# A fused encoder layer with 32 experts: down-projection chunks placed between gate/up chunks, and both gather halves through one pair of PSUM banks

## What is computed

```python
def moe(h, w_router, b_router, w_gu, b_gu, w_down, b_down):
    logits = (xt @ w_router + b_router).astype(jnp.float32)
    top_vals, top_idx = lax.top_k(logits, TOP_K)          # 4 of 32 experts
    gates = jax.nn.softmax(top_vals, axis=-1).astype(h.dtype)
    ...
    def expert_block(args):
        gu = xblk @ w_gu[e] + b_gu[e]                     # 1024 -> 2048
        x_glu = jnp.minimum(gu[:, :F], SWIGLU_LIMIT)
        x_lin = jnp.clip(gu[:, F:], -SWIGLU_LIMIT, SWIGLU_LIMIT)
        act = x_glu * jax.nn.sigmoid(SWIGLU_ALPHA * x_glu) * (x_lin + 1.0)
        return act @ w_down[e] + b_down[e]                # 1024 -> 1024
    ...
y = rms_norm(x + moe(rms_norm(x, norm_ffn_w), ...), norm_final_w)
```

## Time and profile before

| | us |
|---|---|
| median of 3 runs | 1229.29 (1227.29 to 1232.49) |
| the profiled execution | 1230.21 |
| its span, first to last instruction | 1228.4 |
| PE busy in the span | 1147.9 (93%) |
| DVE busy | 1102.8 (90%) |
| ACT busy | 923.5 (75%) |
| weights and other data moved | 457.80 MB, mean 373 GB/s |

### The profile page before, as it was taken

How to read it: one execution, slowest core, us unless ns; L and a number is a source line. 1 busy time by engine, 2 the same in 40 slices (tenths; PEclk the granted TensorE clock), 3 DMA queues, 4 the chain that set the end, 5 groups by cost and what they waited for, 6 DMA issues and landing times.

```text
span 1228.4 us, 40032 instructions
## 1 busy us (share of the span) xinstructions
PE 1147.9 (93%) x17576; PEld 888.3 (72%) x17577; DVE 1102.8 (90%) x804; ACT 923.5 (75%) x825; POOL 92.2 (8%) x69
## 2 busy tenths in 40 slices
PE   5999999899999999999999999999999999999995
PEld 3444655877878878887877777777777787887852
DVE  5855576989999999999999999999999999999987
ACT  4435345778888888888888888888888888888861
POOL 0110400000240000000000000000000000000320
PEclk9999999999999999999999999999999999999998
DMA  9504873999999999999999999999999999999983
GB/s 348 215 23 172 293 289 148 396 398 408 417 420 420 421 419 421 420 420 420 420 419 420 418 420 420 419 418 419 418 415 416 414 417 420 420 420 403 421 343 160
DMA packets 73143, 457.80 MB, mean 373 GB/s; under 512 B 10034, under 2 KB 10546, under 8 KB 23520
## 3 DMA queue, kind: packets, MB, share of 16 engines
q1 hardware_dynamic: 68480, 445.30, 88.7%
q0 software_dynamic: 3360, 7.93, 1.7%
q10 hardware_dynamic: 1152, 2.19, 0.5%
HBM read 443.26 MB, written 24.38 MB: 381 GB/s over the span
## 4 chain that ended last, share of the span: by engine, by line
PE 81%; DVE 9%; issue 6%; DMA 2%; ACT 2%; DVEq 0%; SPq 0%; ACTq 0%
PE ps L445 36%; PE ps L482 24%; PE ps L1155 8%; PE ps L438 6%; DVE ring L423 4%; PE ps L1258 2%; PE ps L467 1%; DMA arena<-planes 1%; DMA ring<-in_w_in_dram 1%; PE ps L1195 1%; PE ps L1183 1%; DVE arena L1895 0%; DVE ring L1516 0%; DVE arena L1901 0%; PE ps L452 0%
## 5 line engine op out<-in xcount | busy, mean ns | idle before, releaser
L445 PE MATMUL ps<-arena,ring 128*128 128x88 f16 x12288 | 500.5, 205 | 36.5 <-issue 35.2
L445 PEld LDWEIGHTS ps<-arena,ring 128*128 128x128 f16 x12288 | 487.6, 100 | 43.0 <-issue 40.0
L423 DVE SCALAR_TENSOR_TENSOR ring<-ring 128x2048 f16<-128x2048 f32 x196 | 439.6, 2283 | 3.5 <-ACT ring L420 2.9
L423 DVE SCALAR_TENSOR_TENSOR ring<-arena,ring 128x2048 f16<-128x2048 f32 x156 | 353.8, 2286 | 32.1 <-ACT ring L420 32.1
L420 ACT ACTIVATE ring<-ring 128x2048 f16<-128x2048 f32 x196 | 365.1, 1908 | 11.0 <-DMA ring<-in_w_gu_dram 5.0
L482 PE MATMUL ps<-ring,arena 128*88 128x512 f16 x1536 | 337.2, 379 | 0.8 <-issue 0.7
L420 ACT ACTIVATE ring<-arena 128x2048 f16<-128x2048 f32 x156 | 291.1, 1904 | 5.0 <-DMA arena<-in_w_down_dram 2.2
L482 PEld LDWEIGHTS ps<-ring,arena 128*88 128x88 f16 x1536 | 181.9, 120 | 142.3 <-issue 1.1
L504 POOL DMA_INDIRECT planes<-arena,slot_row x30 | 66.4, 2213 | 938.3 <-ACT arena L529 909.1
L529 ACT ACTIVATE arena<-ps,slot_gate 88x512 f32<-88x512 f32 x60 | 37.8, 680 | 94.3 <-PE ps L482 94.3
L438 PE MATMUL ps<-arena 128*128 128x88 f16 x2048 | 92.9, 205 | 10.8 <-issue 10.4
(11 more groups left out here) (171 smaller groups left out, 628.4 us busy)
## 6 DMA issues: line engine op xcount, KB each, us to landing
ring<-in_w_gu_dram SPq DMA_DIRECT2D x130, 1024.0 KB, 19.7
arena<-in_w_gu_dram SPq DMA_DIRECT2D x125, 1024.0 KB, 18.8
ring<-in_w_down_dram SPq DMA_DIRECT2D x66, 1024.0 KB, 19.3
extra<-in_w_down_dram SPq DMA_DIRECT2D x31, 1024.0 KB, 20.3
arena<-in_w_down_dram SPq DMA_DIRECT2D x31, 1024.0 KB, 19.7
ring<-in_w_in_dram SPq DMA_DIRECT2D x4, 2048.0 KB, 12.5
ring<-in_w_out_dram SPq DMA_DIRECT2D x2, 2048.0 KB, 8.5
arena<-planes SPq DMA_DIRECT2D x4, 1024.0 KB, 14.5
```

The costliest lines, as they stand in the source:

```text
L423: return dve.scalar_tensor_tensor(split_of(slot)[:, 1, :], raw(r), SCALE_W, split_of(slot)[:, 0, :], ALU.mult, ALU.subtract)
L445: mm = pe.matmul(o, w[:, i, cols], src[:, j, k, :], start=start and n == 0, stop=stop and n == 2, skip_group_check=True)
```

## The change

The 12 chunks of a stage get a new order, `ORDER`: g0, g1, g2, d0, g3, d1, g4, g5, d2, g6, g7, d3. Loads, `high`, `low` and PE's products all follow it. The silu and the clamp of an expert, which read the finished gate/up sums, now wait for the first 11 chunks of its stage (`GU_END`) and stand in the next stage: ACT's silu behind high 3, DVE's clamp behind low 3. The product follows low 4 and its low part follows low 5; on ACT the rows and the product's high part stand between high 4 and high 5. Both gather halves go through banks 6 and 7 (`MISC`); PE waits before the second until ACT has copied the first. The first two experts' first halves still go through banks 4 and 5 (`BOTH[1]`). Stage 1, written out by hand before, becomes an ordinary stage.

```diff
+    ORDER = ("g0", "g1", "g2", "d0", "g3", "d1", "g4", "g5", "d2", "g6", "g7", "d3")
+    GU_END = 11
...
             def place(h, q, c):
                 s = 2 * h + q
                 slot = raw_slot(h, q, c)
-                ins = load_gu(sp, c, s, slot) if c < GU_CH else load_dn(sp, c - GU_CH, s - 1, slot)
+                k = int(ORDER[c][1])
+                ins = load_gu(sp, k, s, slot) if ORDER[c][0] == "g" else load_dn(sp, k, s - 1, slot)
...
             def stage(h, q, first=False, last=False):      # ScalarE
                 s = 2 * h + q
                 high(h, q, 0)
                 columns(s, q, 0)
                 if not last:
                     slots(s)
-                glu(s - 1, nth(s - 1, GU_CH))
                 high(h, q, 1)
                 high(h, q, 2)
                 high(h, q, 3)
+                glu(s - 1, nth(s - 1, GU_END))
+                high(h, q, 4)
                 finish_rows(s - 2, nth(s, 0), first)
-                high(h, q, 4)
                 act_high_part(s - 1)
-                for c in range(5, 8):
+                for c in range(5, 10):
                     high(h, q, c)
-                high(h, q, 8)
-                high(h, q, 9)
                 if not last:
                     columns(s + 1, 1 - q, 1)
                 high(h, q, 10)
...
             def stage(s, q, last=False, more_meta=True):   # TensorE
                 pe.wait_ge(gu_taken, s)
                 pe.wait_ge(glu_ready, s)
                 pe_bias(pe, s)
                 pe.wait_ge(xT_ready, 2 * s + 2)
-                for k in range(4):
-                    gate_up(s, q, k, k)
+                gate_up(s, q, 0, 0)
+                gate_up(s, q, 1, 1)
+                gate_up(s, q, 2, 2)
+                pe.wait_ge(act_ready, s)
+                if s > 1:
+                    pe.wait_ge(row_ready, 2 * s - 2)
+                down(s, 0, 3)
                 if not last:
                     pe.wait_ge(meta_ready, s + 1)
-                gate_up(s, q, 4, 4)
-                pe.wait_ge(row_ready, 2 * s - 2)
+                    gather(s + 1, 1)
+                gate_up(s, q, 3, 4)
+                down(s, 1, 5)
+                gate_up(s, q, 4, 6)
                 if not last:
-                    gather(s + 1, 1)
-                for k in range(5, KD):
-                    gate_up(s, q, k, k)
-                if not last:
+                    pe.wait_ge(xT_ready, 2 * s + 3)
                     if more_meta:
                         make_meta(s + 1)
                     gather(s + 1, 0)
-                    pe.wait_ge(xT_ready, 2 * s + 3)
-                pe.wait_ge(act_ready, s)
-                for j in range(DN_CH):
-                    down(s, j, GU_CH + j)
+                gate_up(s, q, 5, 7)
+                down(s, 2, 8)
+                gate_up(s, q, 6, 9)
+                gate_up(s, q, 7, 10)
+                down(s, 3, 11)
...
             def next_onehot(e):
                 dve.wait_ge(meta_done, e)
+                dve.wait_ge(gathered, 2 * e)
                 dve_onehot(dve, e, 0).then_inc(onehot_ready, 1)
...
             def stage(h, q, last=False):                   # VectorE
                 s = 2 * h + q
                 low(h, q, 0)
                 low(h, q, 1)
-                multiplied(s - 1)
+                if not last:
+                    next_onehot(s + 1)
                 low(h, q, 2)
                 low(h, q, 3)
-                if not last:
-                    next_onehot(s + 1)
+                taken(s - 1, nth(s - 1, GU_END))
                 low(h, q, 4)
+                multiplied(s - 1)
                 low(h, q, 5)
                 act_low_part(s - 1)
-                for c in range(6, 10):
+                for c in range(6, CH):
                     low(h, q, c)
-                if last:
-                    taken(s, nth(s, GU_CH))
-                    low(h, q, 10)
-                    low(h, q, 11)
-                else:
-                    low(h, q, 10)
-                    taken(s, nth(s, GU_CH))
-                    low(h, q, 11)
```

More of the change, by code:

```diff
@@ L427, in build_program @@
         MISC = ps[:, 6:8, :]
+        BOTH = (ps[:, 6:8, :], ps[:, 4:6, :])
         GU = ps[:, 0:4, 0:PER * CAP]
@@ L431, in build_program, with pe_gather @@
         ROWS_LAST = ps[0:CAP, 6:8, :]
-        def pe_gather(pe, i):
+        def pe_gather(pe, i, out_of):
             for d in range(KD):
-                o = (MISC if i == 0 else YT)[:, d // 4, (d % 4) * CAP:(d % 4 + 1) * CAP]
+                o = out_of[:, d // 4, (d % 4) * CAP:(d % 4 + 1) * CAP]
                 for t in range(NT):
@@ L490, in dve_onehot, with act_xT @@
                 ALU.is_equal)
-        def act_xT(act, q, i):
-            src = (MISC if i == 0 else YT)[:, :, 0:4 * CAP]
+        def act_xT(act, q, i, out_of):
+            src = out_of[:, :, 0:4 * CAP]
             return act.activation(xT[:, q, i].rearrange("p (a k) c -> p a (k c)", a=2), src, ACT.Copy)
@@ L967, in _, with columns @@
             act.activation(std[:, 14, 0:1], eps_t[:, :], ACT.Silu)
-            def columns(e, q, i):
+            def columns(e, q, i, out_of=MISC):
                 act.wait_ge(gathered, 2 * e + 2 - i)
-                act_xT(act, q, i).then_inc(xT_ready, 1)
+                act_xT(act, q, i, out_of).then_inc(xT_ready, 1)
             def slots(e):
@@ L977, in slots @@
                 act_slots(act, e, 0, slot_row[0:CAP, bass.ds(e, 1)]).then_inc(meta_ready, 1)
-            columns(0, 0, 1)
+            columns(0, 0, 1, BOTH[1])
             columns(0, 0, 0)
@@ L1036, in _ @@
             high(0, 1, 4)
-            columns(1, 1, 1)
+            columns(1, 1, 1, BOTH[1])
             glu(0, GU_CH, first=True)
@@ L1041, in _ @@
             high(0, 1, 5)
-            high(0, 1, 6)
-            high(0, 1, 7)
             act_high_part(0)
-            high(0, 1, 8)
-            high(0, 1, 9)
+            for c in range(6, 10):
+                high(0, 1, c)
+            columns(2, 0, 1)
             high(0, 1, 10)
             high(0, 1, 11)
-            columns(2, 0, 1)
             stage(1, 0, first=True)
@@ L1056, in _ @@
             stage(E // 2 - 1, 1, last=True)
-            glu(E - 1, nth(E - 1, GU_CH))
             high(E // 2, 0, 0)
+            glu(E - 1, nth(E - 1, GU_END))
+            high(E // 2, 0, 1)
             act_high_part(E - 1, actT_last)
-            high(E // 2, 0, 1)
             act.wait_ge(wg_turned, 2)
@@ L1089, in one @@
                     act.wait_ge(more["gathered"], 2 * n - i)
-                    act_xT(act, 0, i).then_inc(more["xT"], 1)
+                    act_xT(act, 0, i, BOTH[i]).then_inc(more["xT"], 1)
                 act.wait_ge(more["meta_done"], n)
@@ L1308, in _, with gather @@
             warm(1)
-            def gather(e, i):
+            def gather(e, i, out_of=MISC):
                 pe.wait_ge(onehot_ready, e + 1)
-                pe_gather(pe, i).then_inc(gathered, 1)
+                pe_gather(pe, i, out_of).then_inc(gathered, 1)
             def make_meta(e):
@@ L1321, in _ @@
             pe.wait_ge(parts_ready, NT)
-            gather(0, 1)
+            gather(0, 1, BOTH[1])
             emptied(pe, ("pos", 0))
@@ L1370, in _ @@
             gate_up(0, 0, 6, DN_CH + 6)
-            gather(1, 1)
+            gather(1, 1, BOTH[1])
             gate_up(0, 0, 7, DN_CH + 7)
@@ L1375, in _ @@
             gather(1, 0)
[L1376 to L1390, removed]
+            stage(1, 1)
             stage(2, 0)
@@ L1425, in one @@
                 for i in (1, 0):
-                    pe_gather(pe, i).then_inc(more["gathered"], 1)
+                    pe_gather(pe, i, BOTH[i]).then_inc(more["gathered"], 1)
                 pe_bias(pe, e)
@@ L1825, in _ @@
             low(0, 1, 3)
+            multiplied(0)
             low(0, 1, 4)
-            low(0, 1, 5)
-            multiplied(0)
-            low(0, 1, 6)
             next_onehot(2)
-            low(0, 1, 7)
             act_low_part(0)
-            low(0, 1, 8)
-            low(0, 1, 9)
-            low(0, 1, 10)
-            taken(1, nth(1, GU_CH))
-            low(0, 1, 11)
+            for c in range(5, CH):
+                low(0, 1, c)
             stage(1, 0)
@@ L1845, in _ @@
             stage(E // 2 - 1, 1, last=True)
+            low(E // 2, 0, 0)
+            taken(E - 1, nth(E - 1, GU_END))
             multiplied(E - 1)
-            low(E // 2, 0, 0)
+            low(E // 2, 0, 1)
             act_low_part(E - 1, actT_last)
-            low(E // 2, 0, 1)
             low(E // 2, 0, 2)
```

## The result

The changed kernel takes 1331.03 us (median of 4 runs, 1330.58 to 1335.19), the kernel before 1230.26 beside it: ratio 1.0826, 95% interval 1.0806 to 1.0847. The forecast was 1286, with a range to 1318. The direction and the chain were right. Of the other 45 us, some 41 went with the falls of the clock, the mechanism of the rival priced at 1335 (experiment 2 gets them back); the rest is mostly the end.

What follows compares the result with a forecast made beforehand. PE with its gaps and the transfers were taken to bind at about 30.5 us a stage; the chain makes it 32.4. 1230.2 + 56.3 + 0.3 = 1286.8, so a median of 1286 us, range 1266 to 1318.

Steps and rivals of the forecast that it cites:

- the chain: Clamp to first down chunk, over DVE and ACT: now on the path, PE idle over 2 us in each stage.
- the rival priced at 1335: The same as rival C: the clock falls behind the wait before d0, 49 us in all; chance 0.09.
- What bounds the kernel: Stages before: PE with its gaps and the transfers run at the same pace, 30.5 us a stage.
- part 1: PE's order: same 28.7 us of work, slow matmuls mixed among fast ones, issue gaps costed at nothing.
- Rival D: PE's issue gaps stay on the loop, about 1 us in each stage: 29 us, 1315; chance 0.08.
- Parts 2 and 3: Clamp to d0 takes 9.77 us with PE ready at 7.3; the way back to the next clamp makes 32.4 us a stage.
- rival C: Clock falls to half behind the wait before d0, 1.69 us in each of 29 stages: 49 us, 1335; chance 0.09.
- The sum: Whole run: 1230.2 + 56.3 to stage 31's bias + 0.3 for the end = 1286.8, median 1286 us.
- Part 5's end: Behind stage 31's bias: scatter and loads earlier, DVE's last lows later, together +0.3 us, bounds -2 and +2.
- The signs: In the stages: biases 32.4 us apart, PE idle 2.0 to 2.4 us before d0, DMA share well under 1, fewer issue waits.
- Part 4: Both gather halves through one pair of banks: costs nothing, cover 4.8 us.

Runs made afterwards that it cites:

- experiment 2: The changed kernel with 4 spare matmuls (0.86 us) on PE in its wait before the first down chunk: 1289.74 us.
- Experiment 8: The kernel of experiment 5 with the rows moved once more on ACT, behind high 5: 1234.39 us, ratio 1.0027 to the kernel before.
- Experiment 4: The kernel of experiment 2 with 5 more spare matmuls (1.08 us) right behind the first down chunk: 1322.43 us.
- experiment 5: The changed kernel with DVE's product right behind the clamp, its low part behind low 4, and ACT's high part ahead of the rows: 1235.02 us.
- experiment 6: The changed kernel with one move on DVE, the product ahead of low 4 instead of behind it: 1235.89 us.
- experiment 3: The changed kernel with 4 spare matmuls (0.86 us) in PE's other wait, the one before the bias: 1332.20 us.
- experiment 7: The kernel before with only both gather halves put through banks 6 and 7, chunk order as before: 1230.81 us, ratio 0.9999.

## Why the prediction was right and wrong

**What bounds the kernel, and part 1: right.** PE's gaps and the transfers ran at one pace, so nothing could be won. The issue gaps went from 41.2 us to 1.9 us in the stages, without any gain; PE now waits for the chain. Experiment 8 shows the limit from the other side: at 30.01 us a stage by its own chain, the transfers bring it back to 30.7. That the gaps went when slow matmuls came between the fast ones would fit a supply of instructions that fast matmuls outrun, which is not shown. The Trainium skill, Runtime: NRT & Kernel Launch, section Instruction fetch mechanics, calls the fetch mostly hidden. The prediction took the gaps for it; no run here shows the fetch itself, only that the gaps depend on the order, 41.2 us before and 1.9 after. Rival D, that they stay, is out.

**Parts 2 and 3: right, to a tenth.** Foretold: `act_ready` 9.62 us after the clamp's start, d0 at 9.77, the next clamp at 32.43. Measured in the changed kernel, clamp and low part on DVE, then d0 on PE:

```profile
606.92 0.88 DVE L519 TENSOR_SCALAR arena<-ps 128x704 f32<-128x704 f32 x1
...
615.67 0.88 DVE L529 SCALAR_TENSOR_TENSOR arena<-arena 128x704 f16<-128x704 f32 x1
616.48 4.49 DVE L425 SCALAR_TENSOR_TENSOR ring<-arena,ring 128x2048 f16<-128x2048 f32 x2
616.61 4.47 PE L485 MATMUL ps<-ring,arena 128*88 128x512 f16 x12 [2.28 <-DVE arena L529]
```

Low part done at 616.55, 9.63 us after the clamp's start; d0 at 616.61, 9.69. The next clamp came after 32.40 us where the clock held. Experiment 4 shows the loop, experiments 5 and 6 the chain. The bias of stage 31 came in experiment 2, which is nearly the prediction's kernel without the clock, at 1210.5 us; foretold 1210.6. That tenth is luck: stage 2 began 0.8 us earlier than foretold and the last two stages took 0.7 us more.

**The step that failed: rival C against the forecast.** The sum has the wait before d0 (9.77 - 7.3 us) and nothing for a clock that falls behind it. I gave that fall 0.09, on the ground that the one wait of 2.18 us with a fall behind it stood among f32 transposes, and that gaps up to 1.4 us had left the clock at 1.00. But the wait in question was 2.28 us, and the only row with a wait like it showed the fall; the rows against it were all of shorter waits. What the runs showed in place of the nothing is 34.09 - 32.40 = 1.69 us a stage in 23 of the 29 stages, and a somewhat shorter fall in one more. The rival's 1335 us, 4 us from the median, is near in part by luck: it counts 29 falls in the stages, and the end came out 5.6 us longer than foretold.

Two longer waits at the start of the kernel before say less than they seem to:

```profile
15.59 4.14 PE L1155 MATMUL ps<-ring,arena 128*128 128x512 f16 x12 [3.54 <-DVEq L1512]
```
```profile
15.50:19.50 4.00, 3.91 (x12) 1.57 (x13) 3.56 (x8) 2.52 (x4) 0.00 (x0) 1.00 1.04 392
```

Behind the wait of 3.54 us the profile has a granted clock of 1.00, though 12 matmuls take 4.14 us there and 2.75 at 27.04 us. The wait of 10.11 us ahead of the first matmul has 1.00 behind it too. These rows can be read either way.

And the near row was a weaker sign than it looked. The same wait of 2.18 us stands in all twelve profiles of this case, and only those of the kernel before and of experiment 6 show a fall behind it (24 matmuls in 7.03 us); in the other ten they take 5.34. The changed kernel's own profile is one of the ten:

```profile
38.05 0.66 PE L1174 MATMUL ps<-sm,arena 128*128 128x128 f32 x4 [2.18 <-DVE arena L1548]
38.55 5.34 PE L1155 MATMUL ps<-ring,arena 128*128 128x512 f16 x24
```

Before d0 it is otherwise: of the 52 waits of 1.93 us or more in the stages of the changed kernel and of experiment 3 (stage 31's with them), 50 were followed by a fall. So one trace could show that a wait of this length can send the clock down, and not how often: 0.09 was low for so near a row, and the right chance it could not tell.

The Trainium skill, TensorE: Matmul & The Clock Gate, section HAM oscillation, tells of a kernel whose matmuls start at half clock again after every wait for loads. The waits there are longer than those here, so that section alone would not have foretold this fall. The pattern is the one that this trace shows, at 1.93 to 2.28 us: a granted clock of 0.52 behind the wait, 0.96 in the mean over the stages.

**The sum.** In the profiled execution against the one foretold (1286.8 with a span of 1285.0): bias of stage 2 at 267.0 instead of 268.3, -1.3; the stages from there to stage 31's bias 982.1 instead of 942.3, +39.8, by 23 falls of 1.69 in the stages to 1051 us (38.9) and one more behind 1189 us, in a stage of 36.20 us that also holds the last gates (3.8 over 32.40, where the forecast had 2.7 for the gates); behind it 1329.1 - 1249.1 = 80.0 instead of 74.4, +5.6. Together +44.

**Part 5's end: mis-sized.** I gave the end +0.3 us. It was +2.6 in experiment 2, where the clock did not fall there (1287.2 - 1210.5 = 76.7, before 74.1), and +5.9 in the changed kernel (80.0). The difference of 3.3 us is two more falls: 4.26 instead of 2.62 us for the first down chunk of stage 31, and 12.06 instead of 10.39 for the last 48 matmuls. I had followed the scatter and the loads, and they were early: POOL's step of 17.48 us took 1.83 there. But the end had changed hands. The last expert's down chunks start later behind its clamp, and DVE waits for PE's final sums:

```profile
1282.65 12.23 PE L485 MATMUL ps<-ring,arena 128*88 128x512 f16 x48 [2.31 <-DVE arena L529]
...
1301.85 1.23 DVE L1875 TENSOR_TENSOR arena<-ps,arena 128x1024 f32<-128x1024 f32 x1 [6.63 <-PE ps L1441]
```

**The signs: one was misleading.** I said that the DMA share would fall well below 1. It is 0.97 in the mean and 1.00 in a stage of 32.40 us, at 382 and 402 GB/s. The share stays up where the transfers no longer bind; the GB/s and ACT's waits tell it: in the changed kernel's stages none of ACT's waits names DMA. The three largest:

```profile
ACT ring L422 <- PE ps L485: 99.0, 87, 2.4
ACT arena L526 <- DVE arena L523: 76.2, 29, 4.8
ACT ring L422 <- PE ps L448: 28.2, 58, 0.7
```

**Part 4: right** (experiment 7).

## What to carry to other kernels

Where work of one kind is interleaved with work that depends on a chain over three in-order engines, count the chain with everything that is queued between its links: here two 2 us conversions, harmless each, stood between them, and one of them moved past the product was worth 7%. Then ask what a wait does to TensorE's clock: search the trace of before for the waits nearest in length, weigh them more than the many short ones, and look at more than one execution, since the same wait can show the fall in one and not in the next. Where the row is near and the place is passed in every stage, price both cases and let the range hold both. And look for what binds today: the gaps that this order removes hid behind transfers that run at the same pace, so that even the mended order only comes back to where it started.

## What the runs showed that I had not expected

Spare matmuls made a kernel 3% faster: 1331 to 1290 us, by 4 x 0.216 us of useless work a stage.

The falls come in long rows, and length alone doesn't decide. In the changed kernel 23 stages in a row, up to 1051 us, have a wait of 1.93 to 2.28 us and a fall. Then four stages of 32.40 us follow. In the first three a gap named issue, 0.43 to 0.59 us, stands among the gate/up matmuls, and the wait behind it is only 1.51 to 1.68 us. The last of the four has the full wait without a fall:

```profile
1059.74 2.79 PE L485 MATMUL ps<-ring,arena 128*88 128x512 f16 x12 [1.68 <-DVE arena L529]
...
1156.94 2.79 PE L485 MATMUL ps<-ring,arena 128*88 128x512 f16 x12 [2.28 <-DVE arena L529]
...
1159.57 1.42 PE L441 MATMUL ps<-arena 128*128 128x88 f16 x32
```

The chunk's turn is 2.63 us there, against 4.31 in most stages with a fall. The next stage has the same wait and a fall again. In the profile of experiment 3 two stages in the middle are of 32.4 us as well, the first with a wait of 1.20 us, the second with the full 2.28. And a shorter wait does not save the clock there: this one, with an issue gap of 0.46 us just before it, was followed by a fall, as was one of 1.43 us in stage 30:

```profile
309.78 4.39 PE L485 MATMUL ps<-ring,arena 128*88 128x512 f16 x12 [1.66 <-DVE arena L529]
```

In experiment 7's profile, on the other hand, an issue gap of 2.38 us between gate/up matmuls left the clock at 1.00. A wait of about 2 us before d0 makes the fall likely, not certain; what decides between the cases the runs do not settle.
